# A fixed high, low, low, high order for the two widths of matmul in the split-weight projections

## The chip, the core and the metric

The kernel runs on one core of a Trainium2 chip. The metric is the device time of one execution in microseconds (us), as the median of several runs. TensorE (PE in the profile) does the matmuls, VectorE (DVE) and ScalarE (ACT) prepare weights and take results away, SyncE (SP) issues the loads of weights.

## The reference

One layer of a hybrid encoder over 256 frames and 16 meta tokens, model width 2048, in float32. Cut to what matters here:

```python
u = rmsnorm(h, norm_mix_g)
proj = u @ w_in                       # 2048 -> 4 x 1024 + 512 + 256 + 64
rq, rk, rv, rg, cq, ckv, kr = split(proj)
ret_out = silu(rg) * head_groupnorm(retention(rope(rq), rope(rk), rv))
mla_out = rmsnorm(latent_attention(cq, ckv, kr))
h = h + concat([ret_out, mla_out]) @ w_o
m = rmsnorm(h, norm_mlp_g)
h = h + square(relu(m @ w_up)) @ w_down   # 2048 -> 8192 -> 2048
return rmsnorm(h[frames], final_norm_g)
```

## The kernel before

**Split operands.** Every weight chunk (128 x 2048 floats, 1 MB) is loaded to `raw`, rounded by ACT into `hi`, and DVE writes the remainder `raw - hi` to `lo`. Activations are split in the same way: a row of `xs` holds for each of 16 tiles of the contraction (k = 0 to 15) the rounded values and, 272 floats further, their remainders. A product is then made of three terms, high x high, high x rest, rest x high.

**A wide block.** `wide` (L433 is the line of the matmul helper `mm` that it calls) makes one output block of 128 columns of weights against 256 frames. For each k it issues two matmuls. `high(k)` multiplies the tile of `hi` with both parts of the activation at once: two pieces of 256 columns, 512 in all, into the whole PSUM bank `acc`. `low(k)` multiplies the tile of `lo` with the first part, 256 columns, into the second half of the same bank. A block is thus 16 high and 16 low matmuls, all accumulating in one bank; the next block uses the other of the two banks `acc0` and `acc1`, and the other of two buffers of `hi` and `lo`. When a block is done, ACT reads half of the bank into `half_b` and DVE adds the other half (`z<-acc,half_b`), and the block after next may use the bank.

**Where wide blocks run.** There are 84: four for `cq` and 16 for `q` and `gate` in the first part of the kernel, and 64 of the MLP's up projection, 16 in a row at the head of each of four segments (chunks `c0` to `c0 + 15`). The first two of the MLP are cut at k = 12 and end one after the other. What lies between wide blocks is other work of TensorE: narrow blocks of 272 columns, attention, the down projection.

**Order and semaphores.** The loop goes over k in pairs, n = 0, 2, ..., 14. At n = 0 and n = 8 TensorE waits for `lo_ready`, the count of halves of `lo`; at n = 0 also for `acc_read`. After the fourth pair and after the last one the last matmul of the pair adds one to `chunk_used`. ACT waits for it before it writes the half of `hi` of the chunk after next, DVE follows ACT with `lo`, and SP loads the next chunk once DVE is done. The order of TensorE's instructions is the order in which the code is written. In the loop before:

```python
high(n)
if last and n + 2 == KT:
    low(n)
    low(n + 1)
    m = high(n + 1, True)
else:
    high(n + 1)
    low(n)
    m = low(n + 1)
if n % 8 == 6 and not (late and n == 6):
    m.then_inc(sem["chunk_used"], 2 if late else 1)
```

Of the kernel before, what the change touches and what calls it, by code (L numbers as in the profile page):

```python
# [25 lines left out]
KT = D // P  # L26
# [110 lines left out]
def hymba_block(nc, w_in, w_o, w_up, w_down, x_all, x_frames, gains_in, consts_in, gfin_in, out):  # L137
    ctx = ExitStack()
    with ctx:
# [291 lines left out]
        def _(pe):  # L431
            def mm(o, l, m, start=True, stop=True):
                return pe.matmul(o, l, m, start=start, stop=stop)  # L433

            def wide(c, b, wide_of, hi_of, more=0, bmore=0, first=True, last=True, span=(0, KT), ready=None, late=False):

                a = acc[b % 2]
                both = a[:].rearrange("p (a t) -> p a t", a=2)

                def high(k, end=False):  # L440
                    return mm(both, hi[c % 2][:, k * P:k * P + P], wide_of(k), first and k == 0, end)

                def low(k):
                    return mm(a[:, FRAMES:], lo[c % 2][:, k * P:k * P + P], hi_of(k), False, False)

                for n in range(*span, 2):
                    if n % 8 == 0:
                        pe.wait_ge(sem["lo_ready"], 2 * c + n // 8 + 1 + 2 * more)
                    if n == 0 and first and b >= 2:
                        pe.wait_ge(sem["acc_read"], b - 1 + bmore)  # L450
                    if ready is not None:
                        ready(n)
                        ready(n + 1)
                    high(n)
                    if last and n + 2 == KT:
                        low(n)
                        low(n + 1)
                        m = high(n + 1, True)
                    else:
                        high(n + 1)  # L460
                        low(n)
                        m = low(n + 1)
                    if n % 8 == 6 and not (late and n == 6):
                        m.then_inc(sem["chunk_used"], 2 if late else 1)

# [51 lines left out]
            def frames(name, ready=None):  # L517
                wide(CHUNK_OF[name], BLOCK_OF[name], x_wide, x_hi, ready=ready)
# [202 lines left out]
            def product(o, x, w, first, last):  # L721

                mm(o[:], x[0], w[0], first, False)
                mm(o[:], x[0], w[1], False, False)
                return mm(o[:], x[1], w[0], False, last)

            def unit(c, j):
                return hi[c % 2][:, j * GROUP:(j + 1) * GROUP], lo[c % 2][:, j * GROUP:(j + 1) * GROUP]
# [8 lines left out]
            def wo_act(k, t):  # L737
                tile = WO_ORDER[k]
                return hid[:, tile, t * P:t * P + P], hid[:, tile, FRAMES + t * P:FRAMES + t * P + P]
# [13 lines left out]
            for k in range(WO_ALL):  # L753
                c = C_WO + k
                wo_ready(k)
                for g in range(GROUPS):
                    if g % 2 == 0:
                        pe.wait_ge(sem["lo_ready"], 2 * c + g // 2 + 1)
                    for t in range(TILES):
# [7 lines left out]
                        m = product(wo_acc[g][t], wo_act(k, t), unit(c, g), k == 0, False)  # L767
                    if g % 2 == 1:
                        m.then_inc(sem["chunk_used"], 1)
            for g in range(GROUPS):  # L770
                for n in range(WO_PARTS):
# [3 lines left out]
                    for t in range(TILES):  # L775
                        for j in range(PER_CHUNK):
                            wo_ready(k0 + j)
                            m = product(wo_acc[g][t], wo_act(k0 + j, t), unit(c, j), False,
                                        n == WO_PARTS - 1 and j == PER_CHUNK - 1)
# [9 lines left out]
            def act_of(s, n, t):  # L789

                if n < PLAIN:
                    tile = act_p[:, n, :]
                elif s == SEGS - 1 and n % 2 == 0:
                    tile = act_x[:, (n - PLAIN) // 2, :]
                elif n % 2:
                    tile = act_p[:, PLAIN + (n - PLAIN) // 2, :]
                else:
                    assert t == 0
                    i = (n - PLAIN) // 2
                    return act_w[:, i, 0, 0:P], act_w[:, i, 1, 0:P]  # L800
                return tile[:, t * P:t * P + P], tile[:, FRAMES + t * P:FRAMES + t * P + P]
# [48 lines left out]
            for s in range(SEGS):  # L850
# [7 lines left out]
                for j in range(SEG):  # L858
                    if s == 0 and j == 0:
                        ready = KT - PER_CHUNK  # L860
                        pe.wait_ge(sem["m_lo"], 2 * PER_CHUNK)
                        wide(c0, b0, m_wide, m_hi, last=False, span=(0, ready), ready=m_parts)
                        wo_turn(GROUPS - 1)
                        pe.wait_ge(sem["h_ss"], TILES + 1)
                        mm(ps_qn[:, 0:FRAMES], ones, diag[:]).then_inc(sem["h_ss_ps"], 1)
                        wide(c0 + 1, b0 + 1, m_wide, m_hi, last=False, span=(0, ready), late=True)
                        wide(c0, b0, m_wide, m_hi, first=False, span=(ready, KT), ready=m_parts)
                        wide(c0 + 1, b0 + 1, m_wide, m_hi, first=False, span=(ready, KT), late=True)
                    elif s == 0 and j == 1:
                        continue  # L870
                    else:
                        wide(c0 + j, b0 + j, m_wide, m_hi)
# [5 lines left out]
                for d in range(2 * HALF_D if s < SEGS - 1 else HALF_D):  # L878
                    kind, n = mixes[d]
# [17 lines left out]
            for t in range(TILES):  # L897
                for q in range(quads - 2, quads):
                    c = cd + quads + q
                    for j in range(PER_CHUNK):  # L900
                        if j % 2 == 0:
                            pe.wait_ge(sem["lo_ready"], 2 * c + j // 2 + 1)
                        m = product(tail_acc[3][t], act_of(SEGS - 1, PER_CHUNK * q + j, t), unit(c, j), False,
                                    q == quads - 1 and j == PER_CHUNK - 1)
# [1170 lines left out]
```

## Time and profile before

| | us |
|---|---|
| median of three runs | 1095.07 |
| lowest and highest | 1095.05, 1095.15 |
| the profiled execution's own time | 1094.69 |
| its span in the profile | 1092.8 |
| TensorE busy | 1078.6 (99% of the span) |
| VectorE busy | 884.0 |
| ScalarE busy | 671.9 |

The span is the part of the profiled execution in which instructions ran. In the timeline a row gives the start, the time to the modelled end of the last instruction, the engine, the line, the tiles (written <- read), and how many instructions of a kind follow each other (x2). Starts are rounded to 0.01 us. The pitch of a matmul is the distance from its start to the start of the next one. Matmuls overlap, so a pitch is shorter than the duration shown.

### The profile page before, as it was taken

The page shows a single profiled execution, that of the slowest core. Times are in us where ns is not written, and L with a number is a line of the kernel's source. Part 1 is how long each engine was busy: PE and PEld are TensorE (multiplying, and loading weights), DVE is VectorE, ACT ScalarE, POOL GpSimd, SP SyncE. Part 2 cuts the span into 40 slices and gives each one's busy share as a digit, 9 for nine tenths or more (in the row PEclk, how much of TensorE's full clock was granted, in tenths as well). Part 3 has the DMA queues.
Part 4 walks back from the last instruction along what each step waited for, and adds up shares of the span by engine and source line. Part 5 has one row for each costly group of instructions (what it writes and reads, how often), then busy time and mean ns, then how long its engine had stood idle before and what let it go on. Part 6 is the DMA issues. An engine that isn't in the chain of part 4 may idle for free.

```text
span 1092.8 us, 15281 instructions
## 1 busy us (share of the span) xinstructions
PE 1078.6 (99%) x6032; PEld 945.1 (86%) x6032; DVE 884.0 (81%) x1243; ACT 671.9 (61%) x1015; POOL 37.9 (3%) x50
## 2 busy tenths in 40 slices
PE   7999999999999999999999999999999999999997
PEld 7899999999988888888888888888888888888886
DVE  7987988888785567789868879887979896889965
ACT  8665766676654556566655566665556655566644
POOL 0001111111100000000000000000000000000000
PEclk9999999999999999999999999999999999999999
DMA  9544444444465545556655555565555665555751
GB/s 339 213 155 154 158 152 157 153 154 155 154 226 198 193 154 195 190 186 204 223 196 193 193 193 186 200 228 193 187 177 182 227 205 198 184 189 187 263 199 77
DMA packets 30311, 206.88 MB, mean 189 GB/s; under 512 B 3488, under 2 KB 3744, under 8 KB 6048
## 3 DMA queue, kind: packets, MB, share of 16 engines
q1 hardware_dynamic: 29952, 205.59, 53.1%
q8 instruction: 48, 0.79, 0.3%
q10 hardware_dynamic: 288, 0.31, 0.1%
q14 instruction: 23, 0.19, 0.1%
HBM read 203.79 MB, written 2.10 MB: 188 GB/s over the span
## 4 chain that ended last, share of the span: by engine, by line
PE 94%; DVE 3%; ACT 1%; DMA 1%; SPq 1%; issue 0%; ACTq 0%
PE acc L433 59%; PE ps_kn L433 8%; PE ps_v L433 7%; PE ps_x L433 5%; PE ps_qn L433 5%; PE ps_qr L433 5%; PE ps_y L433 5%; DMA raw<-w_in 1%; DVE lo L1319 1%; DVE x_sq L1319 0%; SPq L378 0%; ACT x_sq L961 0%; ACT hi L911 0%; SPq L382 0%; DVE rstdx L1428 0%
## 5 line engine op out<-in xcount | busy, mean ns | idle before, releaser
L1319 DVE TENSOR_TENSOR lo<-raw,hi 128x1024 fp32r<-128x1024 f32 (+2 forms) x381 | 459.6, 1214 | 130.0 <-ACT hi L911 125.9
L433 PE MATMUL acc<-xs,hi 128*128 128x512 f32 (+1 forms) x1952 | 539.0, 361 | 0.1
L911 ACT ACTIVATE hi<-raw 128x1024 fp32r<-128x1024 f32 (+2 forms) x381 | 397.9, 1047 | 217.8 <-PE acc L433 100.1
L433 PE MATMUL acc<-xs,lo 128*128 128x256 f32 (+1 forms) x1648 | 357.5, 284 | 7.0 <-DVE xs L1352 7.0
L433 PEld LDWEIGHTS acc<-xs,lo 128*128 128x128 f32 x1648 | 310.6, 188 | 59.8 <-issue 6.9
L433 PEld LDWEIGHTS acc<-xs,hi 128*128 128x128 f32 x1952 | 309.9, 190 | 3.5 <-issue 0.2
L911 ACT ACTIVATE half_b<-acc 128x256 f32<-128x256 f32 x84 | 32.2, 383 | 113.2 <-PE acc L433 113.1
L433 PE MATMUL ps_kn<-hi,act_p 128*128 128x512 f32 x192 | 74.7, 389 | 0.0
L1319 DVE TENSOR_TENSOR t_raw<-raw 128x1024 f32<-128x1024 f32 (+1 forms) x56 | 53.5, 955 | 1.0
L1319 DVE TENSOR_TENSOR z<-acc,half_b 128x256 f32<-128x256 f32 x64 | 27.1, 423 | 31.0 <-ACT half_b L911 31.0
L1319 DVE TENSOR_TENSOR t_lo<-t_raw,t_hi 128x1536 fp32r<-128x1536 f32 x28 | 49.1, 1752 | 0.0
L433 PE MATMUL acc<-hi,act_p 128*128 128x512 f32 x112 | 43.6, 389 | 0.0
L433 PE MATMUL ps_v<-hi,act_p 128*128 128x512 f32 x112 | 43.6, 389 | 0.0
L433 PE MATMUL ps_y<-hi,act_p 128*128 128x512 f32 x112 | 43.6, 389 | 0.0
L433 PEld LDWEIGHTS ps_kn<-hi,act_p 128*128 128x128 f32 x192 | 36.0, 188 | 7.3
L911 ACT ACTIVATE t_hi<-t_raw 128x1536 fp32r<-128x1536 f32 x28 | 41.3, 1473 | 0.0
L433 PE MATMUL ps_kn<-lo,act_p 128*128 128x512 f32 x96 | 37.4, 389 | 0.0
L1319 DVE TENSOR_TENSOR res<-res,kept 128x1024 f32<-128x1024 f32 (+1 forms) x29 | 32.9, 1146 | 0.2
L1838 DVE SCALAR_TENSOR_TENSOR r<-z,rstd 128x256 f32<-128x256 f32 x64 | 27.1, 424 | 1.8
L1265 ACT ACTIVATE sq<-r 128x256 f32<-128x256 f32 x48 | 20.0, 418 | 8.4 <-DVE r L1838 8.2
L433 PEld LDWEIGHTS acc<-hi,act_p 128*128 128x128 f32 x112 | 21.0, 188 | 4.4
L433 PEld LDWEIGHTS ps_v<-hi,act_p 128*128 128x128 f32 x112 | 21.0, 188 | 4.4
(383 smaller groups left out, 1512.8 us busy)
## 6 DMA issues: line engine op xcount, KB each, us to landing
raw<-w_up SPq DMA_DIRECT2D x64, 1024.0 KB, 4.8
raw<-w_down SPq DMA_DIRECT2D x64, 1024.0 KB, 4.8
raw<-w_in SPq DMA_DIRECT2D x41, 1024.0 KB, 4.8
raw<-w_o SPq DMA_DIRECT2D x16, 1024.0 KB, 4.8
res<-x_frames SPq DMA_DIRECT2D x1, 2048.0 KB, 8.1
raw<-w_in SPq DMA_DIRECT2D x7, 256.0 KB, 7.8
x_in<-x_all SPq DMA_DIRECT2D x3, 544.0 KB, 7.4
consts<-consts_in SPq DMA_DIRECT2D x1, 1218.5 KB, 9.1
```

What stands on the lines that cost most here:

```text
L433: return pe.matmul(o, l, m, start=start, stop=stop)
L911: return act.activation(o, i, ACT.Copy)
L1265: act.activation(sq[:], r[:], ACT.Square)
L1319: return dve.tensor_tensor(o, a, b, op)
L1838: dve.scalar_tensor_tensor(out=r[:], in0=z[:], scalar=0.0, in1=rstd[:], op0=ALU.max, op1=ALU.mult).then_inc(sem["up_r"], 1)
```

## The change

The special case for the last pair goes, and every pair n, n + 1 is issued as high(n), low(n), low(n + 1), high(n + 1). The same 32 matmuls of a block remain, with the same operands, and the same semaphores; only the last pair of a block had this order before.

```diff
                     high(n)
-                    if last and n + 2 == KT:
-                        low(n)
-                        low(n + 1)
-                        m = high(n + 1, True)
-                    else:
-                        high(n + 1)
-                        low(n)
-                        m = low(n + 1)
+                    low(n)
+                    low(n + 1)
+                    m = high(n + 1, last and n + 2 == KT)
```

On TensorE at the joint of two blocks of the up projection (`acc1` to `acc0`; rows of 128x512 are high, rows of 128x256 low matmuls; `xs_56` the activations, `hi0`, `hi1`, `lo0`, `lo1` the weight buffers), before:

```order
L433 MATMUL acc1<-xs_56,hi0_52 128x512 x2
L433 MATMUL acc1<-xs_56,lo0_54 128x256 x2
L433 MATMUL acc1<-xs_56,hi0_52 128x512
L433 MATMUL acc1<-xs_56,lo0_54 128x256 x2
L433 MATMUL acc1<-xs_56,hi0_52 128x512
L433 MATMUL acc0<-xs_56,hi1_53 128x512 [waits acc_read,lo_ready]
L433 MATMUL acc0<-xs_56,hi1_53 128x512
L433 MATMUL acc0<-xs_56,lo1_55 128x256 x2
```

and after:

```order
L433 MATMUL acc1<-xs_56,hi0_52 128x512 x2
L433 MATMUL acc1<-xs_56,lo0_54 128x256 x2
L433 MATMUL acc1<-xs_56,hi0_52 128x512
L433 MATMUL acc0<-xs_56,hi1_53 128x512 [waits acc_read,lo_ready]
L433 MATMUL acc0<-xs_56,lo1_55 128x256 x2
L433 MATMUL acc0<-xs_56,hi1_53 128x512 x2
```

The single high matmul between two pairs of low ones is gone ahead of the joint, and at the joint two high matmuls stand together where there were three.

On TensorE in the middle of a block, where it waits for the second half of `lo`, before:

```order
L433 MATMUL acc1<-xs_56,hi0_52 128x512 x2
L433 MATMUL acc1<-xs_56,lo0_54 128x256 x2
L433 MATMUL acc1<-xs_56,hi0_52 128x512 [waits lo_ready]
L433 MATMUL acc1<-xs_56,hi0_52 128x512
L433 MATMUL acc1<-xs_56,lo0_54 128x256 x2
```

and after:

```order
L433 MATMUL acc1<-xs_56,hi0_52 128x512 x2
L433 MATMUL acc1<-xs_56,lo0_54 128x256 x2
L433 MATMUL acc1<-xs_56,hi0_52 128x512
L433 MATMUL acc1<-xs_56,hi0_52 128x512 [waits lo_ready]
L433 MATMUL acc1<-xs_56,lo0_54 128x256 x2
```

The wait stood between a low and a high matmul, and now stands between two high ones.

## Rows read from the trace of the kernel before

**Rows 1.** The page, busy time by engine, and one group of instructions with its idle time:

```profile
PE 1078.6 (99%) x6032; PEld 945.1 (86%) x6032; DVE 884.0 (81%) x1243; ACT 671.9 (61%) x1015; POOL 37.9 (3%) x50
...
L433 PE MATMUL acc<-xs,lo 128*128 128x256 f32 (+1 forms) x1648 | 357.5, 284 | 7.0 <-DVE xs L1352 7.0
```

**Rows 2.** The page, the chain that ended last, by engine:

```profile
PE 94%; DVE 3%; ACT 1%; DMA 1%; SPq 1%; issue 0%; ACTq 0%
```

**Rows 3.** Timeline of TensorE around a joint: start, us, engine, line, tiles, count:

```profile
446.96 0.40 PE L433 MATMUL acc<-xs,lo 128*128 128x256 f32 x2
447.20 0.62 PE L433 MATMUL acc<-xs,hi 128*128 128x512 f32 x2
...
449.28 0.39 PE L433 MATMUL acc<-xs,hi 128*128 128x512 f32 x1
...
449.75 0.87 PE L433 MATMUL acc<-xs,hi 128*128 128x512 f32 x3
450.45 0.40 PE L433 MATMUL acc<-xs,lo 128*128 128x256 f32 x2
450.69 0.63 PE L433 MATMUL acc<-xs,hi 128*128 128x512 f32 x2
...
451.39 0.39 PE L433 MATMUL acc<-xs,hi 128*128 128x512 f32 x1
```

**Rows 4.** Timeline of TensorE, first and last of twelve blocks, and outermost runs of three:

```profile
26.54 0.87 PE L433 MATMUL acc<-xs,hi 128*128 128x512 f32 x3
...
416.31 0.87 PE L433 MATMUL acc<-xs,hi 128*128 128x512 f32 x3
...
417.95 0.62 PE L433 MATMUL acc<-xs,hi 128*128 128x512 f32 x2
...
421.42 0.39 PE L433 MATMUL acc<-xs,hi 128*128 128x512 f32 x1
...
479.25 0.62 PE L433 MATMUL acc<-xs,hi 128*128 128x512 f32 x2
...
482.72 0.39 PE L433 MATMUL acc<-xs,hi 128*128 128x512 f32 x1
...
483.19 0.87 PE L433 MATMUL acc<-xs,hi 128*128 128x512 f32 x3
...
995.53 0.87 PE L433 MATMUL acc<-xs,hi 128*128 128x512 f32 x3
```

**Rows 5.** Timeline of all engines, a block that starts after 272-column matmuls:

```profile
119.78 0.62 PE L433 MATMUL acc<-xs,hi 128*128 128x512 f32 x2
...
120.06 0.68 DVE L1319 TENSOR_TENSOR qn<-ps_x,qn 128x512 fp32r<-128x512 f32 x1
120.19 0.40 ACT L911 ACTIVATE kn<-ps_kn 128x272 fp32r<-128x272 f32 x1
...
121.17 0.62 PE L433 MATMUL acc<-xs,hi 128*128 128x512 f32 x2
```

**Rows 6.** Timeline of TensorE, the first two blocks of the up projection:

```profile
409.33 0.87 PE L433 MATMUL acc<-xs,hi 128*128 128x512 f32 x3
...
410.75 0.85 PE L433 MATMUL acc<-xs,hi 128*128 128x512 f32 x3
...
411.67 0.63 PE L433 MATMUL acc<-xs,hi 128*128 128x512 f32 x2
```

**Rows 7.** Timeline of TensorE, the last block of the first part, after 272-column matmuls:

```profile
279.41 0.62 PE L433 MATMUL acc<-xs,hi 128*128 128x512 f32 x2
...
280.81 0.62 PE L433 MATMUL acc<-xs,hi 128*128 128x512 f32 x2
```

**Rows 8.** Timeline of ScalarE and VectorE, the split of a half chunk:

```profile
447.46 1.06 ACT L911 ACTIVATE hi<-raw 128x1024 fp32r<-128x1024 f32 x1 [0.80 <-PE acc L433]
...
448.55 1.23 DVE L1319 TENSOR_TENSOR lo<-raw,hi 128x1024 fp32r<-128x1024 f32 x1 [1.02 <-ACT hi L911]
```

**Rows 9.** Twelve blocks: us, busy PE, PEld, DVE, ACT, POOL, granted clock, DMA share, GB/s:

```profile
416.54:483.42 66.88, 66.88 (x386) 58.81 (x384) 48.08 (x76) 39.07 (x64) 0.00 (x0) 1.00 0.56 197
```

## The prediction

> **What bounds the kernel now.** I read the busy times first: TensorE is busy for 1078.6 of 1092.8 us, and its low matmuls into `acc` have 7.0 us of idle time ahead of them in all, all of it one wait near the start [rows 1]. The chain that ended last is 94% TensorE [rows 2]. So a nanosecond that a matmul gives back or costs goes to the end of the kernel, as long as the other engines keep up. The change removes no matmul and adds none. It can act only through the pitch of matmuls, which depends on what stands beside them, and through the moment at which a half chunk is given back. Next I read TensorE's timeline over wide blocks, for the distances between starts; the granted clock is 1.00 there, which is 2.4 GHz [rows 9], so it explains no difference inside these blocks.
>
> **A quad of two high and two low matmuls.** Inside a block the old order is high, high, low, low over and over, and each quad takes the same time. From the third pair of a block to its last pair are five quads: 417.95 to 421.42 in the first of twelve blocks, 479.25 to 482.72 in the last [rows 4]. The twelve differences are 3.47 eight times and 3.46 four times, mean 3.467, so a quad takes 0.6933 us. Eight quads are the 32 matmuls of a block: 5.547 us.
>
> **A block as it is.** The twelve blocks take 483.19 - 416.31 = 66.88 us [rows 4], 5.573 each. That is 0.027 us more than eight quads. Where do they sit? At the joint. From 449.28 (the single high matmul of the last pair) to 451.39 TensorE starts six high and six low matmuls, three quads' worth, which should take 2.08 and take 2.11 [rows 3]. Inside it, the run of three high matmuls lasts 0.87; a pair lasts 0.62, and one pitch more would make 0.85. The pair after it lasts 0.63, then pairs are back at 0.62 [rows 3]. So lateness begins in the run of three and is gone after the second pair of the new block.
>
> **What the new order does at the joint.** In terms of neighbours the new order is the old one shifted by one place. In the middle of a block the sequence is still two high, two low. At the joint, the old order has low, low, HIGH, low, low, then HIGH, HIGH, HIGH. The new one has low, low, then HIGH, HIGH, low, low: two and two throughout, as inside a block. If it is the third high matmul in a row that starts late and keeps its followers late, the new joint has no such place, and a block takes 8 x 0.6933 = 5.547. The timeline has 62 runs of three, the first at 26.54 and the last at 995.53 [rows 4]: 2 between `cq` blocks, 15 in each of the four stretches of the up projection (in the first stretch one of them joins the cut first and second blocks). 62 x 0.027 = 1.65 us when the unrounded 0.0267 is used.
>
> **Why I tie it to the run and not to something else at the joint.** Three other things happen there: the bank changes, TensorE waits for semaphores, and ACT and DVE read the finished bank. A block that starts after 272-column matmuls tells the last apart: DVE reads `ps_x` from 120.06 for 0.68 us and ACT reads `ps_kn` from 120.19, while TensorE goes from 119.78 to 121.17 in 1.39 us for two quads, which is 2 x 0.693; it also changed bank and passed the same waits [rows 5]. The run at 409.33 joins the first block's tail to the second's, with no semaphore wait at the joint, and lasts the same 0.87 [rows 6]. The run at 410.75 lasts 0.85, so its first three start on time, yet the pair at 411.67 is 0.63: the lateness comes behind the third one [rows 6]. Against me: the block at 279.41 starts with a pair, behind 272-column matmuls, and takes 1.40 for its first two quads, 0.01 late [rows 7]. So a run of three is not the only way in, though at 0.01 this is half of what a joint shows.
>
> **The middle of a block.** The wait for `lo_ready` now stands between two high matmuls. Before, it stood between low and high, and the pair behind it lasts 0.62 at 447.20, with no trace of a delay [rows 3]. The nearest row for a wait between two high ones is the block joint, where the whole excess is 0.027. From below: a wait there could gain nothing, as a pair at 0.62 is what all others take. I take 0, because the run at 409.33 is as late without a wait as the others are with one [rows 6], and keep 0.027 for a rival.
>
> **The half chunk given back.** `chunk_used` now goes with the eighth high matmul of the half, where it went with the eighth low one. In the old order the pair of low ones at 446.96 ends at 447.36 [rows 3]. In the new order the last start of that quad is a high matmul, one pitch of 0.23 (a pair's 0.62 less one's 0.39) ahead of the start at 447.20 [rows 3]: 446.97, and it ends 0.39 later at 447.36. ACT, which waited 0.80 for it, starts at 447.46, DVE's `lo` ends at 448.55 + 1.23 = 449.78 [rows 8], and TensorE needs that half when the block after next begins, just behind 449.75 + 5.57 = 455.32. Some 5.5 us of slack hide a shift of 0.01. If that cover were gone, it would cost 0.01 for each of 84 blocks, 0.8 us. SP's next load hangs on DVE's end and moves as little. At a block's end the last four matmuls are the same as before, so the reads of `acc` and what follows them move with the block. In the first and last part of the kernel the work around wide blocks is untouched. With blocks 0.03 us shorter DVE still has room: it is busy for 48.08 of 66.88 us [rows 9].
>
> **Sum.** Joints -1.65, middles 0, hand-backs 0. Against the profiled execution's own time: 1094.69 - 1.65 = 1093.04. The median of the runs shown is 0.38 above that execution, so 1095.07 - 1.65 = 1093.42, which is 0.15% less.
>
> **Rivals.**
> *The joint costs what it costs.* The excess belongs to the start of a block with its new bank, its waits and its readers, in whatever order the first matmuls stand. For it: the late start at 279.41 without a run of three [rows 7]. Against it: the clean start at 119.78 under the same conditions [rows 5]. Then nothing is saved: 1095.07.
>
> *Pitch by width alone.* A high matmul takes a fixed time and a low one too, the order is of no account, and the excess is noise: 1095.07 again. Against it stand pairs of 0.62 and 0.63 and a run of 0.87 with the same instructions [rows 3]. [...]
>
> *Slower: a wait inside a pair of high matmuls is what costs.* At every joint a wait stands between two high ones and is late by 0.027; in the middle of blocks it stands after a low one and is not. The new order puts a wait between two high matmuls in the middle of all 84 blocks: 84 x 0.0267 = +2.24 us, the joints staying as they are, 1097.3. And even if the joints gave back their 1.65 us, a middle that costs more than 0.020 (1.65 / 84) would turn the sign. For it: all joints but one. Against: 409.33, which has no wait and is as late [rows 6].
>
> *A part only.* Two high matmuls across a joint keep some 0.01 of the lateness, as at 279.41: 62 x 0.01 = 0.6 is kept, 1094.0.
>
> **Chances.** Forecast 0.50 (1093.42), a part only 0.14 (1094.0), joint costs what it costs 0.20, width alone 0.04 (both 1095.07), slower 0.07 (1097.3), and 0.05 for what no row shows (0.04 a further gain, 0.01 a loss). The predicted time is 1093.4. The range must take in the forecast, the partial case and both cases of no effect, which hold 0.88; with the rounding of a quad (0.002 for eight, 0.1 us for 62) and 0.2 us for other block starts that may lose their 0.01 it runs from 1093.0 to 1095.3. A measurement of this kernel can tell about 0.2% from no change, 2.2 us. The forecast and all cases of no effect lie within that: 0.88. Faster by more than 0.2% (under 1092.9) would need a third more than all the excess at the joints: 0.04. Slower by more, 0.08.
>
> **What would show it right or wrong.** In the profile after: runs of high matmuls are x2 at all joints with 0.62, none with x3; twelve blocks take 66.56 in place of 66.88; the pair or the low ones behind a joint show no 0.63. If twelve blocks still take 66.88, with 0.63 behind the joint, the first rival holds. If they take 67.2 or so and 0.63 shows in the middle of blocks, the wait does it. TensorE's clock below 1.00 in these blocks, or idle time of TensorE ahead of `hi` or `lo` matmuls, would show that something outside this argument decides.

## The result, and the profile after

The changed kernel takes 1097.86 us in the median of 12 runs (1097.02 to 1098.17), the kernel before 1095.13 in its 12 (1094.62 to 1095.62). The ratio is 1.0023, with a 95% interval of 1.0016 to 1.0031: slower by 2.7 us, where 1.65 us less was forecast. Of the 21 runs of the kernel before that stand beside e1 and e2 below, one took 2193.86 us, and the ratios leave it out.

TensorE's busy time went up by 3.4 us with the same number of instructions (the two profiled executions, 1098.04 and 1094.69 us, are 3.35 apart, some 0.6 more than the medians), and its idle time ahead of these matmuls did not change: 7.0 us before the low ones [rows 1] and now. The page of the changed kernel; columns as in [rows 1]:

```profile
PE 1082.0 (99%) x6032; PEld 946.8 (86%) x6032; DVE 884.4 (81%) x1243; ACT 671.7 (61%) x1015; POOL 37.9 (3%) x50
...
L433 PE MATMUL acc<-xs,hi 128*128 128x512 f32 (+1 forms) x1952 | 544.0, 363 | 0.1
...
L433 PE MATMUL acc<-xs,lo 128*128 128x256 f32 (+1 forms) x1648 | 357.9, 284 | 7.0 <-DVE xs L1347 6.7
```

So no wait is behind it: the matmuls themselves follow each other more slowly. The timeline of TensorE in the up projection of the changed kernel, over a block and its joint (start, us, engine, line, tiles, count; it answers to [rows 3]):

```profile
444.51 0.63 PE L433 MATMUL acc<-xs,hi 128*128 128x512 f32 x2
444.98 0.40 PE L433 MATMUL acc<-xs,lo 128*128 128x256 f32 x2
445.21 0.63 PE L433 MATMUL acc<-xs,hi 128*128 128x512 f32 x2
445.68 0.40 PE L433 MATMUL acc<-xs,lo 128*128 128x256 f32 x2
445.91 0.63 PE L433 MATMUL acc<-xs,hi 128*128 128x512 f32 x2
...
450.11 0.63 PE L433 MATMUL acc<-xs,hi 128*128 128x512 f32 x2
```

There is no run of three any more, as forecast. But now every pair of high matmuls lasts 0.63, where before only the one behind a joint did, and a quad takes 0.70: 444.51, 445.21, 445.91. Eight quads, 444.51 to 450.11, make 5.60. The loss is spread evenly over the whole block. Two rows of the same stretch that are 80 quads apart, which is ten blocks (the first pair of high matmuls behind 416 us and the 81st):

```profile
416.51 0.63 PE L433 MATMUL acc<-xs,hi 128*128 128x512 f32 x2
...
472.51 0.63 PE L433 MATMUL acc<-xs,hi 128*128 128x512 f32 x2
```

56.00 us for ten blocks is 5.600 each, against 5.573 before [rows 4]. A trace has four such stretches of the up projection, and in every run of this document they agree within 0.02 us for ten blocks, so differences of 0.005 us a block can be told from the traces. A block that starts after 272-column matmuls had no run of three to lose, and pays in full. Before, such a block started at 119.78 [rows 5] and the next work of TensorE at 125.33, 5.55 later. The timelines, of before and then of after:

```profile
125.33 0.83 PE L433 MATMUL ps_x<-rq_s,rk_s 128*128 128x256 f32 x6
```

```profile
120.70 0.39 PE L433 MATMUL acc<-xs,hi 128*128 128x512 f32 x1
...
126.31 0.83 PE L433 MATMUL ps_x<-rq_s,rk_s 128*128 128x256 f32 x6
```

It takes 5.61 now. 62 x 0.027 for the blocks behind a joint and 22 x 0.05 for the others make 2.8 us (an estimate, with one block standing for the 22), and the medians are 2.7 apart.

### The profile page after: what moved, and what is told of

The parts are those of the page before. It is cut to its first block, busy times and chain, and to the rows that moved or that the text cites. A ratio compares the mean times of both kernels' runs of the same rounds, so it can differ in the third digit from the quotient of the medians.

```text
span 1096.2 us, 15281 instructions
## 1 busy us (share of the span) xinstructions
PE 1082.0 (99%) x6032; PEld 946.8 (86%) x6032; DVE 884.4 (81%) x1243; ACT 671.7 (61%) x1015; POOL 37.9 (3%) x50
## 4 chain that ended last, share of the span: by engine, by line
PE 97%; DMA 1%; ACT 1%; DVE 0%; SPq 0%; issue 0%; ACTq 0%
PE acc L433 61%; PE ps_kn L433 8%; PE ps_v L433 7%; PE ps_x L433 6%; PE ps_qn L433 5%; PE ps_qr L433 5%; PE ps_y L433 5%; DMA raw<-w_in 1%; ACT hi L906 0%; DVE lo L1314 0%; SPq L378 0%; ACT xs L952 0%; PE ps_kn L601 0%; SPq L382 0%; PE ps_y L636 0%
## 5 line engine op out<-in xcount | busy, mean ns | idle before, releaser
L433 PEld LDWEIGHTS acc<-xs,hi 128*128 128x128 f32 x1952 | 305.0, 190 | 0.8 <-issue 0.3
```

## What can differ when the widths do not

Inside a block both orders run high, high, low, low. What the forecast passed over is which tiles stand in a pair. Before, the two high matmuls of a pair took tiles n and n + 1 of `xs`, an even one and then an odd one. In the new order they take n + 1 and n + 2, odd and then even.

The tiles do not lie alike in memory. A row of `xs` has 272 + 272 floats, 2176 bytes, which is 8.5 times 256 bytes. The frames start 64 bytes into each half, and `xs` starts 128 bytes behind a multiple of 256 (`xs_at = here[0] + LINE // 2`). A high matmul streams two pieces of 256 floats, a low one the first of them. Within 256 bytes the pieces start at:

| tile | first piece | second piece |
|---|---|---|
| even | 192 | 0 |
| odd | 64 | 128 |

**Theory (tiles):** the start addresses of successive pieces decide how fast matmuls follow each other, and at these addresses even before odd is good for a pair. **Rival 1:** one tile streamed twice in a row costs; the new order does that at high(n), low(n) and at low(n + 1), high(n + 1). **Rival 2:** the order of widths, counted from the start of a block and its waits, costs. **Rival 3:** the start of a block has a price of its own.

In all experiments the body of `wide` is written as a list of steps, and the diffs show that list. Every kernel computes all sums of the reference, in another order. The time of a block is read as above, from two rows 80 quads apart, which are shown for each.

## Experiments on the order

**e1: high, high, low, low everywhere.** It changes the joint alone.

```diff
-if last and n + 2 == KT:
-    high(n); low(n); low(n + 1); high(n + 1)
-else:
-    high(n); high(n + 1); low(n); low(n + 1)
+high(n); high(n + 1); low(n); low(n + 1)
```

> The old order high, high, low, low also for the last pair of every block, so that no run of three high matmuls stands at a joint and no single high one ahead of it; the operands inside a block stay as before. Theory (tiles): a high matmul on an odd tile of xs that is followed by a high one on an even tile is what runs late; here every pair of high matmuls is even, odd, so a block takes eight quads of 0.6933 = 5.547 us and the kernel 1.65 us less than before, near 1093.5. Rival 1 (same tile streamed twice in a row): none here either, 5.547. Rival 2 (the width order counted from the start of a block): 5.547. Rival 3 (the start of a block costs whatever its order is): 5.573, no change.

Measured: 1093.57 us in the median of 11 runs, ratio to before 0.9984 (0.9975 to 0.9993). That is 1.70 under the 1095.27 of the kernel before in the same comparison (1.64 with the run of 2193.86 left out), where the forecast's arithmetic for the joint was 1.65.

```profile
416.67 0.62 PE L433 MATMUL acc<-xs,hi 128*128 128x512 f32 x2
...
472.14 0.62 PE L433 MATMUL acc<-xs,hi 128*128 128x512 f32 x2
```

55.47 for ten blocks, 5.547 each, joints included. Rival 3 falls: the start of a block costs nothing by itself.

**e2: the changed kernel's widths with other tiles in the pairs.**

```diff
-for n in pairs of the half: high(n); low(n); low(n + 1); high(n + 1)
+high(h + 1); low(h); low(h + 1)                      # h: first tile of the half
+for n in h + 2, h + 4, ...: high(n); high(n + 1); low(n); low(n + 1)
+high(h)
```

> The changed kernel's sequence of widths (high, low, low, high, high, low, low, ... high, waits at the same places), but with the tiles of the high matmuls shifted within each half of a block, so that every two neighbouring high ones take an even tile and then an odd one: 1, 2 3, 4 5, 6 7, 0, then 9, 10 11, ... 8. Theory (tiles): 5.547 us for a block, 1.65 us less than before. Rival 1 (same tile twice in a row): no low one takes the tile of its high neighbour, 5.547. Rival 2 (the widths' order and its waits): 5.600 as in the changed kernel, 2.5 us more than before.

Measured: 1093.84 us in 11 runs, ratio 0.9988 (0.9979 to 0.9997).

```profile
416.46 0.62 PE L433 MATMUL acc<-xs,hi 128*128 128x512 f32 x2
...
471.93 0.62 PE L433 MATMUL acc<-xs,hi 128*128 128x512 f32 x2
```

5.547 again. The widths stand as in the changed kernel, with one high matmul at either end of a half block and the wait for `lo_ready` between two high ones, and the 5.600 is gone. Rival 2 falls, and with it the slower rival of the prediction: a wait at that place costs nothing.

**e3 and e4: pairs odd, even in two other ways.** e3 takes the changed kernel and exchanges the low ones, e4 takes e1 and reverses every pair.

```diff
-high(n); low(n); low(n + 1); high(n + 1)             # the changed kernel
+high(n); low(n + 1); low(n); high(n + 1)             # e3
-high(n); high(n + 1); low(n); low(n + 1)             # e1
+high(n + 1); high(n); low(n + 1); low(n)             # e4
```

> The changed kernel with its two low matmuls of a pair exchanged: high(n), low(n + 1), low(n), high(n + 1). No two neighbours stream the same tile any more; the pairs of high ones are still odd, even. Theory (tiles, odd before even): a block stays at 5.600 us. Rival 1 (same tile twice in a row): back to 5.547, the kernel 4.4 us under the changed one. Rival 2 (the widths' order): 5.600.

> High, high, low, low throughout as in e1, but each pair reversed: high(n + 1), high(n), low(n + 1), low(n). No same tile twice in a row, pairs of high matmuls odd, even. Theory (tiles, odd before even): 5.600 us for a block or more, the kernel 2.5 us over before. Rival 1 (same tile) and rival 2 (the widths' order): 5.547 as e1.

Measured: 1100.99 us for either, one execution each. The timelines, e3 and then e4:

```profile
416.39 0.64 PE L433 MATMUL acc<-xs,hi 128*128 128x512 f32 x2
...
472.93 0.64 PE L433 MATMUL acc<-xs,hi 128*128 128x512 f32 x2
```

```profile
416.64 0.64 PE L433 MATMUL acc<-xs,hi 128*128 128x512 f32 x2
...
473.17 0.64 PE L433 MATMUL acc<-xs,hi 128*128 128x512 f32 x2
```

56.54 and 56.53 for ten blocks, 5.65 each, more than the changed kernel's 5.600. Neither streams a tile twice in a row, so rival 1 falls. Apart from where a block begins in it, both run the same sequence, odd high, even high, odd low, even low, and both take the same time. The theory had the direction; its number for e3, 5.600, was too low. The kernels are 7.4 us over e1, less than 84 x 0.107 = 9.0. More than half of the difference is in the first part: the up projection of e4 starts 1.2 later than that of e1 (405.17 against 403.97), where the 20 blocks ahead of it would give 2.1.

**e9: only the low pairs reversed.**

```diff
-high(n); high(n + 1); low(n); low(n + 1)             # e1
+high(n); high(n + 1); low(n + 1); low(n)
```

> e1's order with only the pairs of low matmuls reversed: high(n), high(n + 1), low(n + 1), low(n). The changed kernel has the high pairs alone the wrong way round and takes 5.600 us a block, e4 has both and takes 5.653. Theory (each kind of pair has its own price of 0.0067 us a quad, and they add): 5.600, the kernel near 1097.9. Rival (only the high matmuls, with their two pieces, mind the address, and e4 is slow for another reason): 5.547.

```profile
416.37 0.62 PE L433 MATMUL acc<-xs,hi 128*128 128x512 f32 x2
...
471.83 0.62 PE L433 MATMUL acc<-xs,hi 128*128 128x512 f32 x2
```

Measured: 1093.7 us, one execution, 5.546 a block. The expectation fell, and its rival gave the number. In the up projection reversed low pairs alone cost nothing, reversed high pairs alone 0.053 a block (the changed kernel), and both together 0.107. The prices don't add: the whole sequence counts. e9 also streams tile n + 1 twice in a row, which is once more against rival 1.

Order and addresses within a block are not all. In the first part of the kernel, where blocks follow other work, the same order at the same addresses does not always take the same time. The timelines, of a block of e9 (its first pair and its last) and then of the block of e3 that corresponds to [rows 7], two pairs six quads apart. (It is called the last of the first part there and is the last but one: one more follows, cut up by other work.)

```profile
66.07 0.62 PE L433 MATMUL acc<-xs,hi 128*128 128x512 f32 x2
...
70.97 0.63 PE L433 MATMUL acc<-xs,hi 128*128 128x512 f32 x2
```

```profile
281.15 0.62 PE L433 MATMUL acc<-xs,hi 128*128 128x512 f32 x2
...
285.31 0.62 PE L433 MATMUL acc<-xs,hi 128*128 128x512 f32 x2
```

In e9 seven quads take 4.90, 0.700 each, where its up projection has 0.693; eight blocks of its first part run so. In e3 six quads take 4.16, 0.693 each, where its up projection has 0.707. That the work ahead of a block sets this is likely, as order, addresses and waits are the same, but it was not shown. The prices of this document are those of the long stretches of the up projection.

**e10: one reversed pair of high matmuls in a block.**

```diff
-high(4); high(5); low(4); low(5)
+high(5); high(4); low(4); low(5)
```

> e1's order with one single pair of high matmuls reversed in a block, tiles 5 and 4, far from the joint of two blocks. The joint of the kernel before holds one such change of addresses and is late by 0.027 us, while in the changed kernel the steady price is 0.0067 for each quad. Theory (a single break of the sequence costs what the joint did, because it takes some matmuls to fall back into step): a block takes 5.57 us. Rival (each reversed pair costs its steady share, the joint's excess had something more in it): 5.553.

Measured: 1094.66 us, one execution. Ten blocks, and then a stretch with pairs that are late:

```profile
416.48 0.62 PE L433 MATMUL acc<-xs,hi 128*128 128x512 f32 x2
...
472.08 0.62 PE L433 MATMUL acc<-xs,hi 128*128 128x512 f32 x2
```

```profile
446.36 0.62 PE L433 MATMUL acc<-xs,hi 128*128 128x512 f32 x2
...
447.05 0.63 PE L433 MATMUL acc<-xs,hi 128*128 128x512 f32 x2
...
448.44 0.63 PE L433 MATMUL acc<-xs,hi 128*128 128x512 f32 x2
...
449.14 0.62 PE L433 MATMUL acc<-xs,hi 128*128 128x512 f32 x2
```

5.560 a block, 0.013 over e1 (84 x 0.013 is the 1.1 us between the two kernels): half of what the old joint had, and twice the steady price of a quad (0.0067), so neither number given beforehand. The reversed pair is that at 446.36 (the block starts at 444.97). The pair behind it lasts 0.63 and another does two quads later, without a run of three anywhere: one break in the sequence makes some matmuls late, and then the rhythm is back. The old joint broke the sequence at more places: high(14) ahead of low(14), low(15) ahead of high(15), and high(15), odd, ahead of high(0), even. That these together make its 0.027 is argued from e1 and e10 and was not shown one by one.

## Experiments on the addresses

**e5 and e6: `xs` moved by 128 bytes.** This exchanges the starts of even and odd tiles, 64 and 128 for even ones, 192 and 0 for odd ones. The order stays that of e1 in e5 and that of e4 in e6.

```diff
-xs_at = here[0] + LINE // 2
+xs_at = here[0]
```

> e1's order (high, high, low, low, all pairs even, odd) with xs moved down by 128 bytes and nothing else, so that even tiles start where odd ones did within a line of 256 bytes and the other way round. Theory (the start address of what is streamed decides, and the tile's number only through it): the pairs now have the addresses of e4, a block takes 5.653 us, the kernel near 1101. Rival (the tile's number or the weights' side decides, or the previous order of work): 5.547, near 1093.6.

> e4's order (every pair odd, even) with xs moved down by 128 bytes. Theory (address): the pairs now have the addresses of e1, a block takes 5.547 us. Rival (the tile's number): 5.653 as e4.

Measured, one execution each: e5 1101.29 us, e6 1093.61 us. The timelines, e5 and then e6:

```profile
416.23 0.64 PE L433 MATMUL acc<-xs,hi 128*128 128x512 f32 x2
...
472.76 0.64 PE L433 MATMUL acc<-xs,hi 128*128 128x512 f32 x2
```

```profile
416.22 0.62 PE L433 MATMUL acc<-xs,hi 128*128 128x512 f32 x2
...
471.69 0.62 PE L433 MATMUL acc<-xs,hi 128*128 128x512 f32 x2
```

5.653 and 5.547. With one constant changed, the best order became the worst and the worst the best, at the very times of e4 and e1. Weights, PSUM banks, semaphores and loads are as they were; what is placed behind `xs` moves down by 256 bytes with it and keeps its place within 256. The start address of what is streamed decides, and the tile's number only through it. The changed kernel's order with `xs` moved in this way would have the starts of e9 and should take its 5.546; it was not run.

**e7 and e8: rows that all start alike.** The rows of `xs` get 288 + 288 floats, 9 times 256 bytes. e7 has e1's order, e8 the changed kernel's.

```diff
-LO = TOK        # 272
+LO = 288
```

> e1's order with the rows of xs 288 + 288 floats long in place of 272 + 272, a whole number of 256-byte lines, so that all tiles start at the same place in a line. No theory says what a block takes at these addresses. Theory (address): whatever it is, e8 in the changed kernel's order takes the same.

> The changed kernel's order (high, low, low, high) with rows of xs of 288 + 288 floats, as e7. Theory (address): a block takes what it takes in e7, to 0.005 us. Rival (tile number, same tile twice in a row, or place of the pair in the block): it is 0.05 us over e7, as the changed kernel is over e1.

```profile
416.70 0.62 PE L433 MATMUL acc<-xs,hi 128*128 128x512 f32 x2
...
472.70 0.62 PE L433 MATMUL acc<-xs,hi 128*128 128x512 f32 x2
```

```profile
416.56 0.63 PE L433 MATMUL acc<-xs,hi 128*128 128x512 f32 x2
...
472.56 0.63 PE L433 MATMUL acc<-xs,hi 128*128 128x512 f32 x2
```

Both take 56.00 for ten blocks, 5.600 each. Where the starts of tiles do not differ, the two orders are equal to the resolution of the trace, and both have the slower value. The whole kernels took 1097.24 and 1098.28, one execution each; the 1.0 between them is not in these blocks. Most of it is there before them: the matmul `ps_x<-x_sq,consts` behind the `cq` blocks starts at 32.48 in e7 and at 33.29 in e8. The 12 runs of the changed kernel are themselves up to 1.15 apart.

**e11 and e12: other places.** e11 starts every piece at a multiple of 256 bytes, with rows of 320 + 320 floats. e12 moves `xs` up by 64 bytes with rows as before. Both have e1's order.

```diff
-LO = TOK                              # e11 alone
+LO = 320
-xs_at = here[0] + LINE // 2           # both
+xs_at = here[0] + LINE - META * 4
```

> e1's order with rows of 320 + 320 floats and xs placed so that every streamed piece starts at the beginning of a 256-byte line. No row so far has such addresses. If it is the crossing of lines that costs, this has the fewest and is faster than 5.547 us a block; if it is the way in which the addresses follow each other (e7 with all tiles alike took 5.600), it is not faster, 5.547 to 5.653.

> e1's order and row length with xs moved up by 64 bytes: even tiles start at 0 and 64 within a line, odd ones at 128 and 192, where they started at 192 and 0, 64 and 128. If only the steps from one piece to the next matter, all steps are those of e1: 5.547 us a block. If the place in the line matters by itself, another value.

The timelines, e11 and then e12:

```profile
416.43 0.62 PE L433 MATMUL acc<-xs,hi 128*128 128x512 f32 x2
...
472.16 0.63 PE L433 MATMUL acc<-xs,hi 128*128 128x512 f32 x2
```

```profile
416.21 0.62 PE L433 MATMUL acc<-xs,hi 128*128 128x512 f32 x2
...
471.68 0.62 PE L433 MATMUL acc<-xs,hi 128*128 128x512 f32 x2
```

e11 takes 5.573 a block and 1093.87 us in all, e12 5.547 and 1093.58 us, one execution each. Pieces that all start at a multiple of 256 bytes are not the fastest, so the number of such boundaries crossed does not by itself set the time. And tiles that all start alike take 5.573 here and 5.600 in e7, so where they start matters and not only that they are alike. e11 as a whole is only 0.3 us over e1, where 84 x 0.027 would be 2.2: its up projection starts at 403.00, that of e1 at 403.97. What gained is the narrow blocks of the first part, which stream rows of `xs` too. One low and two high matmuls of 272 columns repeat there; a low one and the thirteenth low one behind it, in e1 and then in e11:

```profile
286.97 0.29 PE L433 MATMUL acc<-xs,lo 128*128 128x272 f32 x1
...
291.85 0.28 PE L433 MATMUL acc<-xs,lo 128*128 128x272 f32 x1
```

```profile
286.09 0.28 PE L433 MATMUL acc<-xs,lo 128*128 128x272 f32 x1
...
290.90 0.29 PE L433 MATMUL acc<-xs,lo 128*128 128x272 f32 x1
```

Thirteen repeats take 4.88 in e1 and 4.81 in e11, 0.375 and 0.370 each, and there are over 260 of them, worth some 1.3 us (an estimate). Of these two places, that of e1 is better for wide blocks and that of e11 for narrow ones.

e1, e5 and e12 have the same order and the same steps from piece to piece, and differ only in where the whole lies: 5.547 at 0, 5.653 moved by -128, 5.547 moved by +64. So the steps alone do not decide, against what e12 by itself would suggest; the place counts too. By what rule a sequence of starts becomes a time stays open.

## Why the prediction was wrong

- **What bounds the kernel**: right. TensorE's pitch went to the end of the kernel, and no wait appeared.
- **A block as it is**: right. Quads of 0.6933, and 62 joints late by 0.027.
- **The step that failed** stands in the part on the joint: "In terms of neighbours the new order is the old one shifted by one place. In the middle of a block the sequence is still two high, two low", and from it that a block takes 8 x 0.6933. The neighbours were compared by width alone. They are other tiles, at other addresses, and a quad of them takes 0.700. e2 has the same widths with the tiles paired as before and takes 5.547; e5 and e6 show that it is the addresses, by swapping 5.547 and 5.653. Missing in the sum was a term of 84 blocks x 8 quads x 0.0067 = 4.5 us; with the -1.65 of the joints it makes +2.8, and 2.7 was measured.
- **The joint**: the size was right, and e1 collected it. The cause named, a third high matmul in a row, was not shown: e10 has late pairs without one. The block at 279.41 that was 0.01 late without a run of three [rows 7] was the hint, and it was put aside as small.
- **The readers of PSUM and the semaphores at a joint** were rightly ruled out [rows 5, 6]; in e1 both are still there and the joint costs nothing.
- **The middle of a block**: that a wait between two high matmuls costs nothing holds, since e2 has it in all middles. The slower rival gave 1097.3, near the result by luck, by a mechanism that isn't there: its 0.027 would sit behind the middle, while after the change each quad takes 0.70.
- **Pitch by width alone** fell. The Trainium skill, TensorE: Matmul & The Clock Gate, section Back-to-back issue gap, gives the gap of an isolated matmul by its columns only, and says that in a stream of weight loads and matmuls both set the spacing. These runs show more than that: with the same columns and the same weight loads they have 5.547, 5.560, 5.573, 5.600 and 5.653 us for 32 matmuls.
- **The hand-back of a half chunk**: no cost appeared, with TensorE's idle time unchanged.
- **The range** failed because every case left the quad at 0.6933, and the only one above the range with a time of its own, the slower rival, had a chance of 0.07. The question that no case asked is what changes for each instruction besides its kind.

## What to carry to other kernels

When TensorE is the bound and an edit only permutes matmuls, compare old and new neighbours operand by operand, with their start addresses, before calling the steady state unchanged; where rows are not a whole number of 256 bytes long, try both orders of even and odd rows. Measure the period over many repeats: two rows 80 quads apart resolve 0.1 to 0.2 ns of a quad from starts that are rounded to 10 ns. Here e1, the plain high, high, low, low throughout, beats both kernels with 1093.57 us.

## What the runs showed of the hardware

- The pitch of these float32r matmuls depends on where in 256 bytes the streamed operands of successive matmuls start. The same 16 high and 16 low ones took 5.547 to 5.653 us, 1.9% apart; the granted clock over twelve blocks of the changed kernel is 1.00, as in [rows 9]:

```profile
416.54:483.42 66.88, 66.88 (x384) 58.62 (x383) 47.70 (x75) 39.53 (x65) 0.00 (x0) 1.00 0.56 199
```

- Sequence and place both count: high pairs reversed 5.600, low pairs reversed 5.546, both reversed 5.653, the whole moved by -128 bytes 5.653, by +64 bytes 5.547, all tiles alike at 192 and 64 within 256 bytes 5.600, all pieces on a multiple of 256 bytes 5.573.
- One break in a good sequence costs 0.013 us and is over some three quads later (e10).
- A block's own order and addresses do not fix its pace alone: quads of 0.700 in eight blocks of e9's first part and of 0.693 in its up projection, of 0.693 in one block of e3's first part and of 0.707 in its up projection.
- The narrow blocks mind the place of `xs` too: three matmuls of 272 columns take 0.370 in e11 and 0.375 in e1.
- In a profile such lateness is no idle time. It shows in TensorE's busy time (1078.6 before, 1082.0 after, 1077.5 in e1, for the same 6032 instructions), in pairs that last 0.63 or 0.64 in place of 0.62, and in fewer matmuls in a fixed window (386 in 66.88 us before [rows 9], 384 after). The busy time of the group `acc<-xs,hi` alone misleads: its page has 533.9 for e1 and 537.8 for e2, whose blocks take the same 5.547.
